# Latent attention on one Trainium2 core: probabilities transposed in two halves of 64 queries, with TensorE's four passes written out

## The chip, the cores and the metric

The kernel runs on one core of a Trainium2 chip. The metric is device time in microseconds (us), lower is better. The engines are TensorE (PE in the rows; PEld is its weight load), VectorE (DVE), ScalarE (ACT), GpSimd (POOL) and the DMA queues that SyncE (SP) feeds. They run side by side and wait for each other on semaphores. TensorE multiplies a stationary tile (loaded first, a "weight load") with a moving tile and writes to PSUM, which has eight banks (`ps_all[:, 0..7, :]`, 512 fp32 columns each); ScalarE and VectorE read PSUM.

## The reference, cut to what matters

The whole program is two transformer blocks at a width of 1024, with 512 tokens and, in the second block, 256 context tokens. The change concerns one stage only, the latent attention (`mla_mixer`) at the start of the second block, with 16 heads:

```python
def dense_attention(q_lat, q_ctx, k_lat, v_lat, k_ctx, v_ctx):
    ...
        s = jnp.concatenate([jnp.einsum('bqhd,bkhd->bhqk', qc, k_ctx),
                             jnp.einsum('bqhd,bkhd->bhqk', ql, k_lat)], -1)
        p = softmax_f32(s.astype(jnp.float32) * scale).astype(v_lat.dtype)
        return (jnp.einsum('bhqk,bkhd->bqhd', p[..., :n_ctx], v_ctx)
                + jnp.einsum('bhqk,bkhd->bqhd', p[..., n_ctx:], v_lat))

def ctx_attention(q, k, v):
    s = jnp.einsum('bqhd,bkhd->bhqk', q, k).astype(jnp.float32) * q.shape[-1] ** -0.5
    p = softmax_f32(s).astype(v.dtype)
    return jnp.einsum('bhqk,bkhd->bqhd', p, v)
```

The 512 latent queries see 256 context keys and 512 latent keys (768 keys). The 256 context queries see the 256 context keys. A query and key have 64 plain and 32 rotated dimensions, a value has 64.

## The kernel before

The program is a list of stages. Each engine runs its own instruction stream in a written order, and counting semaphores tie the streams together. The stage "mla" has four passes of four heads each. A pass first makes queries, keys and values from the compressed inputs, and then goes through twelve *pairs* (`MLA_PAIRS`). A pair is two heads (`g` = 0 and 1) with one block of 128 queries: for each of two head pairs (`hp`) four latent blocks with 768 keys (pairs 0 to 3 and 6 to 9) and two context blocks with 256 keys (4, 5, 10 and 11).

A pair goes through these steps:

- `scores(n)` on TensorE writes the scores of both heads to banks 0 to 3. The two heads stand in different halves (64 rows) or quarters (32 rows) of the array's rows.
- `most(n, g)` on VectorE takes the row maximum. `exps(n, g)` on ScalarE makes the exponentials `prob` and their sum. `shares(n, g)` on VectorE writes `diag`, a 128 by 128 diagonal of 1 over the sum.
- `turn(n, g)` on TensorE multiplies each 128 by 128 block of `prob` (stationary) with `diag` (moving), which transposes and normalises in one go. A latent head has six blocks. Before the change the first three go to bank 4 and the last three to bank 5, and a context head has two blocks in bank 4 alone.
- `copy(n, g)` brings the result to `prob_t` in SBUF: ScalarE copies bank 4 (semaphore `copied0`), VectorE bank 5 (`copied1`).
- `weigh(n)` on TensorE multiplies `prob_t` with the values.

TensorE's order is `scores(n + 1)`, `weigh(n - 1)`, `turn(n, 0)`, `turn(n, 1)`. ScalarE's is `exps(n + 1, 0)`, `copy(n, 0)`, `exps(n + 1, 1)`, `copy(n, 1)`. VectorE's is `most(n + 1, 0)`, `most(n + 1, 1)`, `copy(n, 0)`, `shares(n + 1, 0)`, `shares(n + 1, 1)`, `copy(n, 1)`. A turn may write a bank when the previous head's copy out of that bank is done.

On every engine the first three passes are one hardware loop and the last pass is written out (`Chain.loop`). In the loop the value of a wait comes from registers.

In the rows, L1545 to L1551 are the latent `scores` and L1540 and L1542 the context ones; L1562 and L1567 are `turn` into banks 4 and 5, L1582 is `weigh`, L1068 `exps`, L1078 ScalarE's copy, L2281 and L2282 `most`, L2261 and L2262 `shares`, and L2292 VectorE's copy. One fp32 matmul of the program is two records in the trace, each with its own weight load, so that "x6" is three matmuls. L1738 is a sum in another stage, whose moving tile is one column wide.

Of the kernel before, what the change touches and what calls it, by code (L numbers as in the profile page):

```python
# [238 lines left out]
def mla_step(a):  # L239
    wq, wkv = weight_panels(a["mla_w_qb_2"][0]), weight_panels(a["mla_w_kvb_2"][0])  # L240
    n = NH // PER
    pairs, units, lat = PER // 2 * 6, PER * 6, PER * 4

    def dma(i, j):

        w, per, first, second = ((wq, DQ, NOPE, ROPE), (wkv, P, NOPE, HD))[j]
        out = []
        for h in range(PER):
            out.append((("cols", h * first, first), w[:, :, ds(i * (PER * per) + h * per, first)]))
            out.append((("cols", PER * first + h * second, second), w[:, :, ds(i * (PER * per) + h * per + first, second)]))  # L250
        return out

    return dict(kind="mla", iters=n, shapes=[(3, PER * DQ), (2, PER * P)], dma=dma,
                totals=dict(q_mm=2 * n, q_out=3 * n, rot_mm=n, q_rot=n, key_mm=2 * n, val_mm=n, kv_out=4 * n,
                            s_made=pairs * n, s_max=units * n, s_exp=units * n, s_shared=units * n,
                            turned0=units * n, turned1=lat * n, copied0=units * n, copied1=lat * n,
                            s_weighted=pairs * n, s_kept=PER * n))
# [121 lines left out]
def build(nc, a, out, upto=99, probe=False):  # L379
# [133 lines left out]
    diag = sb("diag", [P, 2, 2, P], at=g_raw_at + 6144)  # L513
    prob_t = sb("prob_t", [P, 2, T], at=spare)
    prob = (sb("prob_even", [P, 2, T], at=spare + 6144), sb("prob_odd", [P, 2, T], at=g_raw_at + 8192))
    o_lat = sb("o_lat", [P, KD, S], at=hid)
# [515 lines left out]
    MLA_PAIRS = [(hp, ctx, q) for hp in range(PER // 2) for ctx, n in ((0, 4), (1, 2)) for q in range(n)]  # L1032
    MLA_LAT = [2 * sum(1 for u in MLA_PAIRS[:n] if not u[1]) for n in range(len(MLA_PAIRS))]

    def mla_act(st, b, act, split_hi, i, last):
        base_of = lambda name, per: b[name] + i * per
        U, LU = 2 * len(MLA_PAIRS), 4 * PER

# [18 lines left out]
        def exps(n, g):  # L1057
            hp, ctx, q = MLA_PAIRS[n]
            act.wait_ge(sem["s_max"], base_of("s_max", U) + 2 * n + g + 1)
            if n >= 2:  # L1060

                act.wait_ge(sem["turned0"], base_of("turned0", U) + 2 * n + g - 3)
                if not MLA_PAIRS[n - 2][1]:
                    act.wait_ge(sem["turned1"], base_of("turned1", LU) + MLA_LAT[n - 2] + g + 1)
            at = 8 * (n % 2) + 4 * g
# [5 lines left out]
        def copy(n, g):  # L1071
            hp, ctx, q = MLA_PAIRS[n]
            act.wait_ge(sem["turned0"], base_of("turned0", U) + 2 * n + g + 1)
            if n >= 1:

                act.wait_ge(sem["s_weighted"], base_of("s_weighted", len(MLA_PAIRS)) + n)
            W = (2 if ctx else 3) * P
            nc.scalar.activation(prob_t[:, g, 0:W], ps_all[:, 4, 0:W], ACT.Copy).then_inc(sem["copied0"], 1)  # L1078

# [382 lines left out]
    def mla_pe(st, b, pe, triple, i):  # L1462
        base_of = lambda name, per: b[name] + i * per
        U, LU = 2 * len(MLA_PAIRS), 4 * PER
        p0 = st["p0"]
# [88 lines left out]
        def turn(n, g):  # L1554
# [5 lines left out]
            pe.wait_ge(sem["copied0"], base_of("copied0", U) + u)  # L1560
            for t in range(2 if ctx else 3):
                ins = nc.tensor.matmul(ps_all[:, 4, t * P:(t + 1) * P], prob[n % 2][:, g, t * P:(t + 1) * P], diag[:, n % 2, g, :], start=True, stop=True)  # L1562
            ins.then_inc(sem["turned0"], 1)
            if not ctx:
                pe.wait_ge(sem["copied1"], base_of("copied1", LU) + MLA_LAT[n] + g)
                for t in range(3, 6):
                    ins = nc.tensor.matmul(ps_all[:, 5, (t - 3) * P:(t - 2) * P], prob[n % 2][:, g, t * P:(t + 1) * P], diag[:, n % 2, g, :], start=True, stop=True)  # L1567
                ins.then_inc(sem["turned1"], 1)

        def weigh(n):  # L1570

            hp, ctx, q = MLA_PAIRS[n]
            pe.wait_ge(sem["copied0"], base_of("copied0", U) + 2 * n + 2)
            if not ctx:
                pe.wait_ge(sem["copied1"], base_of("copied1", LU) + MLA_LAT[n] + 2)
            if q == 0 and hp == 1:
# [118 lines left out]
    def _(pe):  # L1695
# [123 lines left out]
        for st in PLAN:  # L1819
# [168 lines left out]
            elif kind == "mla":  # L1988
                Chain(pe, None).loop(st["iters"], 0, lambda i, last: mla_pe(st, b, pe, triple, i))
            elif kind == "na":  # L1990
# [275 lines left out]
    def mla_dve(st, b, dve, ch, i):  # L2266
        V = nc.vector
        base_of = lambda name, per: b[name] + i * per
        U, LU = 2 * len(MLA_PAIRS), 4 * PER
        dve.wait_ge(sem["rot_mm"], base_of("rot_mm", 1) + 1)  # L2270
# [13 lines left out]
        def copy(n, g):  # L2284
            hp, ctx, q = MLA_PAIRS[n]
            if ctx:
                return
            dve.wait_ge(sem["turned1"], base_of("turned1", LU) + MLA_LAT[n] + g + 1)
            if n >= 1:

                dve.wait_ge(sem["s_weighted"], base_of("s_weighted", len(MLA_PAIRS)) + n)
            V.tensor_copy(prob_t[:, g, 3 * P:T], ps_all[:, 5, 0:3 * P]).then_inc(sem["copied1"], 1)  # L2292

# [297 lines left out]
```

## Time and profile before

| | |
|---|---|
| median of 3 runs | 4306.83 us (4305.85 to 4313.46) |
| profiled execution, its own time | 4306.24 us |
| span of its trace | 4304.5 us |
| mean granted TensorE clock | 0.959 of full speed |
| TensorE matmul busy | 3925.6 us (91% of the span) |
| VectorE, ScalarE, GpSimd busy | 2144.8, 1398.0 and 1505.0 us |

The span runs from the first to the last instruction of the trace, and the profiled execution's own time has 1.7 us more around it. Busy time counts pipelined matmuls by their modelled ends, so that 91% does not mean a full array. The latent attention's pairs run in four stretches between 2194 and 2591 us.

### The profile page before, as it was taken

Reading aid. Unit: us, or ns where it says so; the run is one execution under the profiler, and the core shown is the slowest. Engines: PE = TensorE matmul, PEld = TensorE weight load, DVE = VectorE, ACT = ScalarE, POOL = GpSimd, SP = SyncE. Lnnn points to the kernel's source line nnn. Section 1 sums busy time; section 2 is a strip of 40 time slices with the busy share of each in tenths; the row PEclk is TensorE's granted clock in tenths of the full one; section 3 lists DMA queues with packets and bytes.
Section 4 is the critical chain, followed back from the end, with each engine's and each line's share of the span. In section 5 each row is a group of like instructions: output and inputs, shape, how many; then the busy total and the mean of one; then the engine's idle time right before and its main releaser. Section 6 shows DMA issues by size and latency. Waiting matters only on the chain.

```text
span 4304.5 us, 56639 instructions
## 1 busy us (share of the span) xinstructions
PE 3925.6 (91%) x20925; PEld 3254.3 (76%) x20925; DVE 2144.8 (50%) x3528; ACT 1398.0 (32%) x1862; POOL 1505.0 (35%) x494
## 2 busy tenths in 40 slices
PE   6999979999999978999989998799968889888997
PEld 5888868888888867888866667578758878767885
DVE  6344855445444677565454445776752332334232
ACT  3322343223412332312333331332234433234232
POOL 1443323343444321444310003344346633234441
PEclk9999989999999988999989998999979999999998
DMA  5454514444453323443300003244414422212221
GB/s 180 142 159 136 148 55 140 139 152 139 144 157 111 118 68 113 139 152 109 76 16 11 19 1 108 78 123 148 139 54 141 137 55 63 68 51 68 88 94 53
DMA packets 551756, 440.60 MB, mean 102 GB/s; under 512 B 60332, under 2 KB 549821, under 8 KB 551357
## 3 DMA queue, kind: packets, MB, share of 16 engines
q1 hardware_dynamic: 551613, 438.67, 33.1%
q8 instruction: 93, 1.52, 0.2%
q14 instruction: 50, 0.41, 0.0%
HBM read 431.58 MB, written 2.83 MB: 101 GB/s over the span
## 4 chain that ended last, share of the span: by engine, by line
PE 70%; DVE 14%; issue 7%; ACT 4%; DMA 2%; POOL 1%; SPq 1%; DVEq 0%; ACTq 0%; POOLq 0%
PE ps_all L1814 19%; PE ps_all L1816 18%; PE ps_all L1815 18%; DVE acc L2376 3%; PE ps_all L1562 2%; PE ps_all L1582 1%; PE ps_all L1879 1%; DMA g_raw<-in_w_mod_dram 1%; PE ps_all L1664 1%; PE ps_all L1567 1%; PE ps_all L1545 1%; DVE full_t L2433 1%; PE ps_all L1549 1%; ACT w_hi L1174 1%; POOL w_lo L789 1%
## 5 line engine op out<-in xcount | busy, mean ns | idle before, releaser
L789 POOL TENSOR_TENSOR w_lo<-raw,w_hi 128x2048 fp32r<-128x2048 f32 (+4 forms) x326 | 1343.1, 4121 | 2352.2 <-ACT w_hi L1174 2252.2
L1814 PE MATMUL ps_all<-h_hi,w_hi 128*128 128x512 f32 (+1 forms) x2704 | 1072.6, 397 | 43.9 <-POOL h_lo L795 34.9
L1815 PE MATMUL ps_all<-h_lo,w_hi 128*128 128x512 f32 (+1 forms) x2704 | 1059.1, 392 | 0.0
L1816 PE MATMUL ps_all<-h_hi,w_lo 128*128 128x512 f32 (+1 forms) x2704 | 1058.8, 392 | 0.0
L1174 ACT ACTIVATE w_hi<-raw 128x2048 fp32r<-128x2048 f32 (+4 forms) x320 | 537.8, 1681 | 1599.1 <-PE ps_all L1816 1424.6
L1814 PEld LDWEIGHTS ps_all<-h_hi,w_hi 128*128 128x128 f32 x2704 | 517.9, 192 | 156.4 <-issue 26.9
L2376 DVE SCALAR_TENSOR_TENSOR acc<-g_raw,c_col,acc 128x256 f32<-128x256 f32 x1104 | 618.2, 628 | 1.7
L1816 PEld LDWEIGHTS ps_all<-h_hi,w_lo 128*128 128x128 f32 x2704 | 516.9, 191 | 106.9
L1815 PEld LDWEIGHTS ps_all<-h_lo,w_hi 128*128 128x128 f32 x2704 | 517.8, 192 | 102.7 <-issue 1.0
L1814 PE MATMUL ps_all<-hid_hi,w_hi 128*128 128x512 f32 (+1 forms) x1272 | 482.3, 379 | 28.9 <-DVE hid_lo L2454 18.9
L1815 PE MATMUL ps_all<-hid_lo,w_hi 128*128 128x512 f32 (+1 forms) x1272 | 474.0, 373 | 0.0
L1816 PE MATMUL ps_all<-hid_hi,w_lo 128*128 128x512 f32 (+1 forms) x1272 | 473.9, 373 | 0.0
L1814 PEld LDWEIGHTS ps_all<-hid_hi,w_hi 128*128 128x128 f32 x1272 | 244.5, 192 | 73.0 <-DVE hid_lo L2454 21.0
L2454 DVE TENSOR_TENSOR hid_lo<-prod_t,hid_hi 128x1024 f32 (+3 forms) x77 | 229.2, 2977 | 110.7 <-ACT hid_hi L1268 110.7
L2451 DVE TENSOR_TENSOR prod_t<-gate_t,ps_all 128x1024 f32<-128x1024 f32 x44 | 53.8, 1222 | 449.7 <-PE ps_all L1816 449.7
L1816 PEld LDWEIGHTS ps_all<-hid_hi,w_lo 128*128 128x128 f32 x1272 | 244.8, 192 | 41.3
L1815 PEld LDWEIGHTS ps_all<-hid_lo,w_hi 128*128 128x128 f32 x1272 | 245.1, 193 | 40.2 <-issue 1.0
L2471 DVE SCALAR_TENSOR_TENSOR x<-ps_all,modc,x 128x512 f32 (+1 forms) x92 | 68.9, 748 | 316.0 <-PE ps_all L1816 315.9
L2378 DVE TENSOR_SCALAR acc<-g_raw,c_col 128x256 f32<-128x256 f32 x240 | 91.0, 420 | 125.2 <-DMA g_raw<-in_ada_w_dram 32.1
L1814 PE MATMUL ps_all<-c_hi,w_hi 128*128 128x256 f32 x400 | 120.1, 300 | 27.2 <-POOL w_lo L789 16.3
L2281 DVE TENSOR_REDUCE stat<-ps_all 128x1 f32<-128x768 f32 (+1 forms) x96 | 74.8, 779 | 125.9 <-PE ps_all L1551 114.4
L2225 DVE SCALAR_TENSOR_TENSOR prod_t<-ps_all,colv,prod_t 128x511 f32<-128x511 f32 (+1 forms) x66 | 40.6, 656 | 177.2 <-ACT prod_t L1263 177.2
(341 smaller groups left out, 5205.1 us busy)
## 6 DMA issues: line engine op xcount, KB each, us to landing
raw<-in_w_ffn_gu_dram SPq DMA_DIRECT2D x88, 1024.0 KB, 5.1
g_raw<-in_w_mod_dram SPq DMA_DIRECT2D x72, 1024.0 KB, 5.1
raw<-in_ffn_w_in_dram SPq DMA_DIRECT2D x66, 1024.0 KB, 5.1
g_raw<-in_ada_w_dram SPq DMA_DIRECT2D x48, 1024.0 KB, 5.3
raw<-in_w_ffn_down_dram SPq DMA_DIRECT2D x32, 768.0 KB, 4.8
raw<-in_w_ffn_down_dram SPq DMA_DIRECT2D x32, 640.0 KB, 4.4
raw<-in_ffn_w_out_dram SPq DMA_DIRECT2D x24, 768.0 KB, 4.8
raw<-in_ffn_w_out_dram SPq DMA_DIRECT2D x24, 640.0 KB, 4.4
```

The source lines that it names most:

```text
L789: nc.gpsimd.tensor_tensor(v(w_lo), v(raw), v(w_hi).bitcast(F32), ALU.subtract).then_inc(sem["w_split_lo"], 1)
L1174: nc.scalar.activation(w_view(w_hi, j % 2, st["shapes"][j]), w_view(raw, j % 2, st["shapes"][j]), ACT.Copy).then_inc(sem["w_split_hi"], 1)
L1562: ins = nc.tensor.matmul(ps_all[:, 4, t * P:(t + 1) * P], prob[n % 2][:, g, t * P:(t + 1) * P], diag[:, n % 2, g, :], start=True, stop=True)
L1814: nc.tensor.matmul(o, whi, mhi, start=first, stop=False)
L1815: nc.tensor.matmul(o, whi, mlo, start=False, stop=False)
L1816: return nc.tensor.matmul(o, wlo, mhi, start=False, stop=last)
L2281: ch.link(V.tensor_reduce(s_(0), pair[:, C:C + (C if ctx else T)], AX_X, ALU.max))
L2376: ins = nc.vector.scalar_tensor_tensor(o, w, s, o, ALU.mult, ALU.add)
L2378: ins = nc.vector.tensor_scalar(o, w, s, None, ALU.mult)
L2451: nc.vector.tensor_tensor(prod_t[:, :, 0:N], gate_t[:, :, 0:N], other, ALU.mult).then_inc(sem["product"], 1)
L2454: nc.vector.tensor_tensor(hid_lo[:, w].rearrange("p (c n) -> p c n", c=2), prod_t[:, :, 0:N], hid_hi[:, w].rearrange("p (c n) -> p c n", c ...
L2471: nc.vector.scalar_tensor_tensor(v, ps_d[:, j, 0:N], modc[:, ds(st["gate"] + j + i * 2, 1)], v, ALU.mult, ALU.add).then_inc(sem[f"down{j}" ...
```

## The change

In `turn`, each 128 by 128 block is now turned in two halves of 64 queries: rows 0 to 63 of `prob` with the upper left 64 by 64 of `diag`, and rows 64 to 127 with the lower right one. The first half (`qh` = 0) goes to bank 4, the second to bank 5, for all six blocks of a latent head and the two of a context head. ScalarE copies the first halves of all blocks from bank 4, VectorE the second halves from bank 5; `half_t` is the view of `prob_t` with every other run of 64 columns. Both banks now carry every head, so each turn and each `weigh` waits for both copies of the head before, and VectorE copies in context pairs too. On TensorE alone, the four passes are written out one after the other without a hardware loop; the other engines keep theirs.

```diff
 def mla_act
-            W = (2 if ctx else 3) * P
-            nc.scalar.activation(prob_t[:, g, 0:W], ps_all[:, 4, 0:W], ACT.Copy).then_inc(sem["copied0"], 1)
+            t = 2 if ctx else 6
+            nc.scalar.activation(half_t(g, 0, t), ps_all[:, 4, 0:t * HD].rearrange("p (t q) -> p t q", q=HD), ACT.Copy).then_inc(sem["copied0"], 1)
 def mla_pe, turn
             pe.wait_ge(sem["copied0"], base_of("copied0", U) + u)
-            for t in range(2 if ctx else 3):
-                ins = nc.tensor.matmul(ps_all[:, 4, t * P:(t + 1) * P], prob[n % 2][:, g, t * P:(t + 1) * P], diag[:, n % 2, g, :], start=True, stop=True)
-            ins.then_inc(sem["turned0"], 1)
-            if not ctx:
-                pe.wait_ge(sem["copied1"], base_of("copied1", LU) + MLA_LAT[n] + g)
-                for t in range(3, 6):
-                    ins = nc.tensor.matmul(ps_all[:, 5, (t - 3) * P:(t - 2) * P], prob[n % 2][:, g, t * P:(t + 1) * P], diag[:, n % 2, g, :], start=True, stop=True)
-                ins.then_inc(sem["turned1"], 1)
+            pe.wait_ge(sem["copied1"], base_of("copied1", U) + u)
+            for t in range(2 if ctx else 6):
+                for qh in range(2):
+                    rows_ = slice(qh * HD, (qh + 1) * HD)
+                    ins = nc.tensor.matmul(ps_all[:, 4 + qh, t * HD:(t + 1) * HD], prob[n % 2][rows_, g, t * P:(t + 1) * P], diag[rows_, n % 2, g, rows_], start=True, stop=True)
+                    if t == (1 if ctx else 5):
+                        ins.then_inc(sem[f"turned{qh}"], 1)
 weigh
-            if not ctx:
-                pe.wait_ge(sem["copied1"], base_of("copied1", LU) + MLA_LAT[n] + 2)
+            pe.wait_ge(sem["copied1"], base_of("copied1", U) + 2 * n + 2)
 tensor block
-                Chain(pe, None).loop(st["iters"], 0, lambda i, last: mla_pe(st, b, pe, triple, i))
+                for i in range(st["iters"]):
+                    mla_pe(st, b, pe, triple, i)
 def mla_dve, copy
-            if ctx:
-                return
-            V.tensor_copy(prob_t[:, g, 3 * P:T], ps_all[:, 5, 0:3 * P]).then_inc(sem["copied1"], 1)
+            t = 2 if ctx else 6
+            V.tensor_copy(half_t(g, 1, t), ps_all[:, 5, 0:t * HD].rearrange("p (t q) -> p t q", q=HD)).then_inc(sem["copied1"], 1)
```

The order of TensorE's rows around pair 1 of the looped passes was this (L1562 and L1567 are the two heads' turns, L1545 begins the next scores):

```order
L1562 MATMUL ps_all<-diag,prob_odd 128x128 [waits copied0,s_shared]
L1562 MATMUL ps_all<-diag,prob_odd 128x128 x2
L1567 MATMUL ps_all<-diag,prob_odd 128x128 [waits copied1]
L1567 MATMUL ps_all<-diag,prob_odd 128x128 x2
L1562 MATMUL ps_all<-diag,prob_odd 128x128 [waits copied0,s_shared]
L1562 MATMUL ps_all<-diag,prob_odd 128x128 x2
L1565 REGISTER_ALU
L1567 MATMUL ps_all<-diag,prob_odd 128x128 [waits copied1]
L1567 MATMUL ps_all<-diag,prob_odd 128x128 x2
L1533 REGISTER_ALU
L1545 MATMUL ps_all<-kn,qn 128x512 [waits s_exp]
```

In the changed kernel the same place reads as follows (L1564 is the turn, L1544 the scores):

```order
L1564 MATMUL ps_all<-diag,prob_odd 128x64 [waits copied1,copied0,s_shared]
L1564 MATMUL ps_all<-diag,prob_odd 128x64 x11
L1564 MATMUL ps_all<-diag,prob_odd 128x64 [waits copied1,copied0,s_shared]
L1564 MATMUL ps_all<-diag,prob_odd 128x64 x11
L1544 MATMUL ps_all<-kn,qn 128x512 [waits s_exp]
```

Six matmuls of 128 moving columns per head have become twelve of 64. The wait for the bank 5 copy, which stood in the middle of a head's turn, has moved to its front beside the wait for the bank 4 copy, and the register work is gone.

On VectorE, between the maxima and the shares of the context pairs, nothing was copied before (L2282 ends `most`, L2261 begins `shares`):

```order
L2281 TENSOR_REDUCE stat<-ps_all 128x1 [waits s_shared,s_made]
L82 REGISTER_ALU
L2282 TENSOR_SCALAR stat<-stat 128x1 [waits dve_chain]
L2260 REGISTER_ALU
L2261 RECIPROCAL stat<-stat 128x1 [waits s_exp]
```

Now a copy of 128 columns stands between them, and another behind the shares:

```order
L2279 TENSOR_REDUCE stat<-ps_all 128x1 [waits s_shared,s_made]
L82 REGISTER_ALU
L2280 TENSOR_SCALAR stat<-stat 128x1 [waits dve_chain]
L2289 COPY prob_t<-ps_all 128x2x64 [waits s_weighted,turned1]
L2258 REGISTER_ALU
L2259 RECIPROCAL stat<-stat 128x1 [waits s_exp]
```

## Rows read from the trace of the kernel before

**Rows 1.** The page: the chain that ended last, share of the span by engine.
```profile
PE 70%; DVE 14%; issue 7%; ACT 4%; DMA 2%; POOL 1%; SPq 1%; DVEq 0%; ACTq 0%; POOLq 0%
```

**Rows 2.** Windows, pass 3: length; busy PE, PEld, DVE, ACT, POOL; clock; DMA.
```profile
2407.00:2486.00 79.00, 72.23 (x593) 51.63 (x594) 37.15 (x106) 29.93 (x73) 2.34 (x1) 0.98 0.04 13
```

**Rows 3.** Timeline of PE (start us, length us), one latent pair of pass 4.
```profile
2560.59 1.13 PE L1545 MATMUL ps_all<-kn,qn 64*128 64x512 f32 x4
...
2563.57 1.53 PE L1582 MATMUL ps_all<-prob_t,vals 128*64 128x128 f32 x24
2565.03 0.94 PE L1562 MATMUL ps_all<-diag,prob_odd 128*128 128x128 f32 x6
...
2566.63 0.91 PE L1562 MATMUL ps_all<-diag,prob_odd 128*128 128x128 f32 x6
...
2568.15 1.13 PE L1545 MATMUL ps_all<-kn,qn 64*128 64x512 f32 x4
```

**Rows 4.** Timeline of PE and PEld: one-column matmuls; four loads into two row halves.
```profile
687.23 1.39 PE L1738 MATMUL ps_all<-mean_m,squares 128*128 128x1 f32 x12
2204.20 0.30 PEld L1545 LDWEIGHTS ps_all<-kn,qn 64*128 64x128 f32 x4
```

**Rows 5.** Groups of PE and PEld, 2150 to 2620 us, by form: busy us, mean ns.
```profile
L1567 PE MATMUL ps_all<-diag,prob_odd 128*128 128x128 f32 x192 | 26.7, 276 | 0.0
L1567 PEld LDWEIGHTS ps_all<-diag,prob_odd 128*128 128x128 f32 x192 | 24.0, 192 | 0.0
L1582 PEld LDWEIGHTS ps_all<-prob_t,vals 128*64 128x64 f32 x896 | 47.9, 137 | 18.8 <-issue 15.5 <-ACT prob_t L1078 3.3
```

**Rows 6.** Timeline of a looped pass, all engines: turns and copies of one pair.
```profile
2209.41 0.83 PE L1567 MATMUL ps_all<-diag,prob_odd 128*128 128x128 f32 x6
2209.69 0.49 ACT L1078 ACTIVATE prob_t<-ps_all 128x384 f32<-128x384 f32 x1
2210.28 0.56 DVE L2292 COPY prob_t<-ps_all 128x384 f32<-128x384 f32 x1 [0.77 <-PE ps_all L1567]
2210.33 0.91 PE L1562 MATMUL ps_all<-diag,prob_odd 128*128 128x128 f32 x6
```

**Rows 7.** Groups of ACT and DVE, 2150 to 2620 us: ScalarE's short copy, VectorE's diagonal.
```profile
L1078 ACT ACTIVATE prob_t<-ps_all 128x256 f32<-128x256 f32 x32 | 12.2, 382 | 17.8 <-PE ps_all L1562 17.8
L2262 DVE TENSOR_SCALAR diag<-ident,stat 128x128 f32<-128x128 f32 x96 | 27.6, 287 | 3.6 <-DVE stat L2261 0.2
```

**Rows 8.** Timeline of PE: context pairs 4 and 5 of pass 1, then scores.
```profile
2228.11 0.71 PE L1562 MATMUL ps_all<-diag,prob_even 128*128 128x128 f32 x4
2229.46 0.68 PE L1562 MATMUL ps_all<-diag,prob_even 128*128 128x128 f32 x4 [0.64 <-ACT prob_t L1078]
...
2233.64 0.71 PE L1562 MATMUL ps_all<-diag,prob_odd 128*128 128x128 f32 x4
2235.76 0.68 PE L1562 MATMUL ps_all<-diag,prob_odd 128*128 128x128 f32 x4 [1.41 <-ACT prob_t L1078]
2236.55 2.05 PE L1545 MATMUL ps_all<-kn,qn 64*128 64x512 f32 x4
```

**Rows 9.** Windows: the stretch that begins with those scores.
```profile
2236.60:2240.00 3.40, 3.40 (x10) 1.62 (x12) 0.38 (x2) 0.26 (x1) 0.00 (x0) 0.50 0.02 5
```

**Rows 10.** Timeline of PE: second scores and last weighing of passes 2, 3, 4.
```profile
2310.04 1.13 PE L1545 MATMUL ps_all<-kn,qn 64*128 64x512 f32 x4
2380.92 0.66 PE L1582 MATMUL ps_all<-prob_t,vals 128*64 128x128 f32 x8 [0.47 <-ACT prob_t L1078]
2415.86 1.13 PE L1545 MATMUL ps_all<-kn,qn 64*128 64x512 f32 x4
2485.10 0.66 PE L1582 MATMUL ps_all<-prob_t,vals 128*64 128x128 f32 x8 [0.47 <-ACT prob_t L1078]
2521.23 1.13 PE L1545 MATMUL ps_all<-kn,qn 64*128 64x512 f32 x4
2589.73 0.66 PE L1582 MATMUL ps_all<-prob_t,vals 128*64 128x128 f32 x8 [0.47 <-ACT prob_t L1078]
```

More of the change, by code:

```diff
@@ L241, in mla_step @@
     n = NH // PER
-    pairs, units, lat = PER // 2 * 6, PER * 6, PER * 4
+    pairs, units = PER // 2 * 6, PER * 6
     def dma(i, j):
@@ L255, in mla_step @@
                             s_made=pairs * n, s_max=units * n, s_exp=units * n, s_shared=units * n,
-                            turned0=units * n, turned1=lat * n, copied0=units * n, copied1=lat * n,
+                            turned0=units * n, turned1=units * n, copied0=units * n, copied1=units * n,
                             s_weighted=pairs * n, s_kept=PER * n))
@@ L514, in build @@
     prob_t = sb("prob_t", [P, 2, T], at=spare)
+    half_t = lambda g, h, n: prob_t[:, g, 0:n * P].rearrange("p (t h q) -> p h t q", h=2, q=HD)[:, h, :, :]
     prob = (sb("prob_even", [P, 2, T], at=spare + 6144), sb("prob_odd", [P, 2, T], at=g_raw_at + 8192))
@@ L1032, in build @@
     MLA_PAIRS = [(hp, ctx, q) for hp in range(PER // 2) for ctx, n in ((0, 4), (1, 2)) for q in range(n)]
-    MLA_LAT = [2 * sum(1 for u in MLA_PAIRS[:n] if not u[1]) for n in range(len(MLA_PAIRS))]
     def mla_act(st, b, act, split_hi, i, last):
         base_of = lambda name, per: b[name] + i * per
-        U, LU = 2 * len(MLA_PAIRS), 4 * PER
+        U = 2 * len(MLA_PAIRS)
         act.wait_ge(sem["q_mm"], base_of("q_mm", 2) + 1)
@@ L1062, in exps @@
                 act.wait_ge(sem["turned0"], base_of("turned0", U) + 2 * n + g - 3)
-                if not MLA_PAIRS[n - 2][1]:
-                    act.wait_ge(sem["turned1"], base_of("turned1", LU) + MLA_LAT[n - 2] + g + 1)
+                act.wait_ge(sem["turned1"], base_of("turned1", U) + 2 * n + g - 3)
             at = 8 * (n % 2) + 4 * g
@@ L1463, in mla_pe @@
         base_of = lambda name, per: b[name] + i * per
-        U, LU = 2 * len(MLA_PAIRS), 4 * PER
+        U = 2 * len(MLA_PAIRS)
         p0 = st["p0"]
@@ L2268, in mla_dve @@
         base_of = lambda name, per: b[name] + i * per
-        U, LU = 2 * len(MLA_PAIRS), 4 * PER
+        U = 2 * len(MLA_PAIRS)
         dve.wait_ge(sem["rot_mm"], base_of("rot_mm", 1) + 1)
@@ L2285, in copy @@
             hp, ctx, q = MLA_PAIRS[n]
[L2286 to L2288 removed]
+            dve.wait_ge(sem["turned1"], base_of("turned1", U) + 2 * n + g + 1)
             if n >= 1:
                 dve.wait_ge(sem["s_weighted"], base_of("s_weighted", len(MLA_PAIRS)) + n)
[L2292 removed]
+            t = 2 if ctx else 6
+            V.tensor_copy(half_t(g, 1, t), ps_all[:, 5, 0:t * HD].rearrange("p (t q) -> p t q", q=HD)).then_inc(sem["copied1"], 1)
         def shares(n, g):
```

## The prediction

> **What bounds the kernel now.** I read the chain that ended last first: TensorE makes 70% of it [rows 1]. Then I read the stage that the change touches. In pass 3 TensorE is busy for 72.23 of 79.00 us, VectorE for 37.15 and ScalarE for 29.93 [rows 2]. So what counts here is TensorE's own stream and the waits in it. The timeline of one latent pair in the written-out pass shows that stream: scores at 2560.59, weighing at 2563.57, the two heads' turns at 2565.03 and 2566.63, the next scores at 2568.15 [rows 3]. The pair takes 7.56 us, and its turns 1.60 + 1.52 = 3.12 us of that. The whole stage has 32 latent pairs and 16 context pairs.
>
> **One head's turn before.** Twelve records of 128 moving columns. A group of six lasts 0.83 us [rows 6] and its last record 0.276 us [rows 5], so the spacing is (0.83 - 0.276) / 5 = 0.11 us, and twelve take 1.33 us. Until the second head's turn starts 1.60 us pass, because it waits for ScalarE's copy of bank 4. Behind the second head 1.52 us pass until the scores.
>
> **One head's turn after.** Twelve matmuls of 64 columns become 24 records, in twelve couples of one upper and one lower half. Two rows say what binds them. Records whose moving tile is one column wide, with the same 128-column stationary tile, come (1.39 - 0.276) / 11 = 0.10 us apart [rows 4], the last record counted as above. So a record with one column costs about what one with 128 costs: the weight load is the limit, and narrower moving tiles gain nothing. Do the two halves' loads run side by side? In the scores, four loads into two row halves take 0.30 us together, with 0.19 us for one [rows 4, 5], so three steps fit into 0.11 us: one step of 0.1 between the two loads of one half, and nothing between the halves. A couple therefore costs one load, 0.11 us, and a head 12 x 0.11 = 1.33 us, as before. I take 1.33.
>
> The Trainium skill says the same of the load (TensorE: Matmul & The Clock Gate, LDWEIGHTS): its time goes with the columns of the stationary tile and not with its rows. The trace agrees: a load of 64 columns takes 137 ns and one of 128 takes 192 [rows 5]. Its page TensorEngine Tiling (Array Packing), Instruction Overhead, warns against taking a tiling factor from a dimension that is already small, and this change takes it from the moving one too.
>
> **The wait.** Before, the second head's turn into bank 4 waited only for ScalarE's copy, which ran while the first head's other half streamed into bank 5. That cover is gone: the last record now fills both banks, and both copies start only then. After the first head's start: last couple at 11 x 0.11 = 1.22 us, its end 0.276 later, 0.04 until VectorE starts (L1567's group ends at 2209.41 + 0.83 = 2210.24, the copy starts at 2210.28), 0.56 for its copy, and 0.11 until TensorE starts (ScalarE's copy ends at 2209.69 + 0.49 = 2210.18, the next turn's load at 2210.30) [rows 6]. That makes 2.21 for 1.60 before. ScalarE's copy is shorter, 0.49, and starts at most 0.1 later, so VectorE's decides. The second head's turn takes 1.33. The 0.19 us beyond it before the scores passed while the array went from 128-row to 64-row tiles; the turn now uses 64-row tiles itself, and I keep 0.02 of them (keeping all of them would add 24 x 0.17 = 4 us). So 2.21 + 1.35 = 3.56 for 3.12, +0.44 us a pair. VectorE is free in time: it had idled 0.77 us before that copy [rows 6]. Behind its copy stand the shares of the next pair, which TensorE needs only after 2.98 us of scores and 1.46 of weighing (2560.59 to 2563.57 to 2565.03) [rows 3]; that cover holds.
>
> Of eight latent pairs in a pass, this hits six. In the first of each head pair (0 and 6) the second turn already stood still for ScalarE, whose copy is queued behind the next exponentials; there I take 0. So 24 x 0.44 = **+10.6 us**.
>
> **Context pairs.** Eight records before, now eight couples at the same spacing. The copy was exposed before too: the second turn starts at 2229.46, 1.35 after the first, with 0.64 idle for ScalarE [rows 8]. ScalarE's copy shrinks from 256 to 128 columns: 0.489 for 384 and 0.382 for 256 [rows 6, 7] give 0.11 us per 128, so 0.27; VectorE's new one of 128 columns takes about 0.29, as its diagonal of that width [rows 7]. Each exposed copy is 0.1 shorter, and before the scores at least another 0.1 goes. With two such savings in each of four pairs, 4 x 0.2 x 4 passes = **-3.2 us**.
>
> **Written-out passes.** From its second scores to its last weighing, pass 3 takes 2485.10 - 2415.86 = 69.24 us in the loop and pass 4 2589.73 - 2521.23 = 68.50 us written out [rows 10]. With the rest of a pass, 0.8 to 0.9 each in three passes: **-2.5 us**. On a longer instruction stream nothing in the trace puts a price; it is fetched during stretches of 100 us.
>
> These sum to 10.6 - 3.2 - 2.5 = +4.9 us.
>
> **The clock.** Pass 2 differs from pass 3 in one thing: its clock fell once behind the context pairs. It takes 2380.92 - 2310.04 = 70.88 us, 1.64 more [rows 10]. In pass 1 the same happened: two short turns with 1.41 us of waiting between them, and the scores behind them take 2.05 us instead of 1.13 [rows 8], at a granted clock of 0.50, which is 1.2 GHz [rows 9]. Two of the eight context groups did this. Such stretches become more and thinner: every steady latent pair now has turn, 0.87 us of waiting, turn, and the array streams half as many columns while it turns. From below this costs nothing. From above, all 24 steady latent pairs and the six other context groups fall once each, 30 x 1.64 = 49 us. I take the six context groups, whose stretch is the nearest to the row that fell, and four of the 24, 10 x 1.64 = **+16 us**.
>
> The sum is +21 us on the profiled execution's own 4306.24, 4327; the median of the runs is 0.6 us above that execution, which changes nothing.
>
> **The rivals.**
>
> *Wait without clock.* The wait comes as above and the clock falls little more often than before: +5 us, 4311. For it: pass 3's context groups did not fall at all. Against: pass 1's and 2's did, with more streaming than will be left.
>
> *The halves really run at twice the rate, and it is faster.* If a couple costs half a load, 0.055, the second head starts 0.60 + 0.99 = 1.59 us after the first (0.99 is the tail and the copy as above), and takes 0.68: 2.27 for 3.12, 24 x -0.85 = -20. The other eight latent pairs give 8 x -0.7 = -6, the context pairs -6, the written-out passes -2.5, some falls of the clock +8: -26, 4280. It decides below 0.09 us a couple, where 2 x 12 x 0.02 us pay for the 0.44. The Trainium skill's page TensorEngine Tiling (Array Packing), Theoretical Speedup, promises up to twofold for a contraction of 64 rows or fewer. For it: the scores of two heads do run together. Against: these scores stream 256 or 512 columns behind each load, and the one-column row puts the load at 0.10.
>
> *The halves' loads run one after the other.* A couple costs 0.22: 32 x 2 x 1.33 = +85 and 32 x 0.44 = +14 for the context turns, with the sum above about +104 before the clock, over 4410. Against it stand the four loads in 0.30 us.
>
> **How the numbers follow.** The wait with a falling clock 0.62, the wait alone 0.18, twice the rate 0.11, serial loads 0.06, something else (a copy that is slower into runs of 64 columns) 0.03. Predicted is the first, 4327 us. The range reaches from just below the second to past all 24 latent pairs falling, 4303 to 4358; outside are the third and fourth and some of the first's tail. What a measurement of this kernel can tell from no change is 0.2%, 8.6 us: faster 0.11 (the third), same 0.19 (the second), slower 0.70.
>
> **What the profile of the changed kernel would show.** The spacing of the turn's records at full clock, by group: 24 records in about 1.5 us is right, 0.9 speaks for twice the rate, 2.9 for serial loads. Between the two heads' turns, idle of some 0.7 us that ends with VectorE's copy. The second turn of a context pair 1.25 us behind the first instead of 1.35. More stretches at a granted clock of 0.50 between 2194 and 2600 us, behind turns. The prediction is wrong if the spacing is not the load's, or if the clock holds.

## The result and the profile after

The changed kernel takes 4381.78 us (median of 4 runs, 4381.18 to 4393.31) where the kernel before takes 4306.69 (4 runs, 4305.85 to 4313.46): a ratio of 1.0177, 95% interval 1.0164 to 1.0189, or 75 us more. The profiled execution's own time is 4381.38 us, its span 4379.6, its mean granted clock 0.941.

Windows of the latent attention from pass 1's first scores to pass 4's last weighing, before and after, then two stretches of the changed kernel in pass 1. The columns are length; busy PE, PEld, DVE, ACT, POOL with their instructions; clock; DMA share; GB/s.

```profile
2187.70:2590.80 403.10, 365.46 (x2781) 266.25 (x2780) 171.01 (x458) 154.40 (x338) 21.51 (x7) 0.96 0.04 10
```

```profile
2184.20:2672.80 488.60, 433.66 (x3677) 319.87 (x3676) 180.28 (x490) 151.67 (x338) 21.51 (x7) 0.78 0.03 9
2213.00:2227.00 14.00, 12.45 (x166) 9.89 (x163) 6.59 (x20) 4.36 (x11) 0.00 (x0) 0.98 0.01 3
2227.00:2233.00 6.00, 6.00 (x44) 4.37 (x42) 1.64 (x5) 1.05 (x3) 0.00 (x0) 0.50 0.00 0
```

The stage grew by 85.5 us and its clock went from 0.96 to 0.78. Summed over the trace's clock records, TensorE stood at half clock for 34 us in 6 stretches before and for 210 us in 24 stretches after, the longest 27.3 us. Outside this stage the profiled execution was 10 us shorter than before, with 310 us at half clock for 322. Over all kernels below, the time outside the stage lay between 3892 and 3910 us. Lengths of the stage therefore tell the small differences better than whole spans do, though each comes from a single profiled execution.

The timeline of PE, one latent pair at full clock in pass 1, which answers to [rows 3], with VectorE's copy between its turns; a context pair that answers to the second of [rows 8]; and the first context pair of pass 4, at full clock (start, length, x records, idle before and what ended it):

```profile
2216.70 1.56 PE L1564 MATMUL ps_all<-diag,prob_even 64*128 64x64 f32 x24
2218.33 0.56 DVE L2289 COPY prob_t<-ps_all 128x384 f32<-128x384 f32 x1 [0.76 <-PE ps_all L1564]
2219.03 1.56 PE L1564 MATMUL ps_all<-diag,prob_even 64*128 64x64 f32 x24 [0.78 <-DVE prob_t L2289]
2220.39 0.68 PE L1539 MATMUL ps_all<-kn,qcn 64*128 64x256 f32 x4
...
2237.80 0.66 PE L1564 MATMUL ps_all<-diag,prob_odd 64*128 64x64 f32 x8
2239.91 0.97 PE L1564 MATMUL ps_all<-diag,prob_odd 64*128 64x64 f32 x8 [1.45 <-DVE prob_t L2289]
...
2607.05 0.66 PE L1564 MATMUL ps_all<-diag,prob_even 64*128 64x64 f32 x8
2608.22 0.66 PE L1564 MATMUL ps_all<-diag,prob_even 64*128 64x64 f32 x8 [0.51 <-DVE prob_t L2289]
2608.68 1.11 PE L1544 MATMUL ps_all<-kn,qn 64*128 64x512 f32 x4
```

The groups of the four copies, which answer to [rows 6, 7]:

```profile
L2289 DVE COPY prob_t<-ps_all 128x384 f32<-128x384 f32 x64 | 35.7, 557 | 69.4 <-PE ps_all L1564 69.4
L1077 ACT ACTIVATE prob_t<-ps_all 128x384 f32<-128x384 f32 x64 | 31.4, 490 | 84.9 <-PE ps_all L1564 84.9
L2289 DVE COPY prob_t<-ps_all 128x128 f32<-128x128 f32 x32 | 9.3, 289 | 31.6 <-PE ps_all L1564 31.6
L1077 ACT ACTIVATE prob_t<-ps_all 128x128 f32<-128x128 f32 x32 | 8.8, 276 | 32.9 <-PE ps_all L1564 32.9
```

At full clock the mechanism is the one forecast. A head's 24 records last 1.56 us and the second head's turn starts 2.33 us after the first, with an idle time of 0.78 that VectorE's copy ends. What the forecast did not see is in the timeline of pass 3, where the clock falls in the middle of a pair; behind it stands the first pair of pass 1, whose turns run at half clock throughout:

```profile
2469.16 1.56 PE L1564 MATMUL ps_all<-diag,prob_even 64*128 64x64 f32 x24
2471.49 2.21 PE L1564 MATMUL ps_all<-diag,prob_even 64*128 64x64 f32 x24 [0.78 <-DVE prob_t L2289]
2473.43 1.24 PE L1539 MATMUL ps_all<-kn,qcn 64*128 64x256 f32 x4
...
2475.75 2.83 PE L1579 MATMUL ps_all<-prob_t,vals 128*64 128x128 f32 x24
2478.51 1.79 PE L1564 MATMUL ps_all<-diag,prob_odd 64*128 64x64 f32 x24
2481.08 1.60 PE L1564 MATMUL ps_all<-diag,prob_odd 64*128 64x64 f32 x24 [0.78 <-DVE prob_t L2289]
2482.44 1.21 PE L1539 MATMUL ps_all<-kn,qcn 64*128 64x256 f32 x4
...
2484.73 2.83 PE L1579 MATMUL ps_all<-prob_t,vals 128*64 128x128 f32 x24
2487.49 1.12 PE L1564 MATMUL ps_all<-diag,prob_even 64*128 64x64 f32 x8
```

```profile
2196.32 2.83 PE L1564 MATMUL ps_all<-diag,prob_even 64*128 64x64 f32 x24
2199.92 2.83 PE L1564 MATMUL ps_all<-diag,prob_even 64*128 64x64 f32 x24 [0.78 <-DVE prob_t L2289]
2202.50 2.06 PE L1544 MATMUL ps_all<-kn,qn 64*128 64x512 f32 x4
```

The weighing takes 2.83 us at half clock instead of 1.53, the context scores 1.24 instead of 0.68. The clock comes back during the turn at 2478.51 (1.79 us long, between the 1.56 of full clock and the 2.83 of half clock) and is gone again one turn later. Of the 24 stretches at half clock, 13 begin in one of the 24 *steady* latent pairs (1, 2, 3, 7, 8 and 9 of a pass), always behind the start of its second turn; before the change none did. Six begin in the context pairs (two before) and five at the start of a pass or in its first pair (four before).

### The profile page after: what moved, and what is told of

Its sections match the earlier page's. It is cut to its first block, busy times and chain, and to the rows that moved or that the text cites. A ratio compares the mean times of both kernels' runs of the same rounds, so it can differ in the third digit from the quotient of the medians.

```text
span 4379.6 us, 58255 instructions
## 1 busy us (share of the span) xinstructions
PE 3987.9 (91%) x21821; PEld 3302.1 (75%) x21821; DVE 2154.8 (49%) x3560; ACT 1395.8 (32%) x1862; POOL 1505.8 (34%) x494
## 3 DMA queue, kind: packets, MB, share of 16 engines
HBM read 431.58 MB, written 2.83 MB: 99 GB/s over the span
## 4 chain that ended last, share of the span: by engine, by line
PE 72%; DVE 13%; issue 7%; ACT 3%; POOL 2%; DMA 1%; SPq 1%; DVEq 0%; ACTq 0%; POOLq 0%
PE ps_all L1811 19%; PE ps_all L1813 18%; PE ps_all L1812 18%; DVE acc L2373 3%; PE ps_all L1564 3%; PE ps_all L1579 2%; POOL w_lo L790 1%; PE ps_all L1876 1%; DMA g_raw<-in_w_mod_dram 1%; PE ps_all L1544 1%; PE ps_all L1661 1%; PE ps_all L1548 1%; DVE full_t L2430 1%; PE ps_all L1720 1%; PE ps_all L1802 1%
```

## The experiments

"Half clock" below is the sum of the clock records at 0.50 inside the stage. The stage's length goes from the first scores of pass 1 to the start of the last record of the last weighing. Each kernel was timed against the kernel before on the same chip; the last column is that ratio with its 95% interval. Beside the experiments the kernel before took 4309 to 4311 us, so ratios and stages compare the rows better than medians do. "Thin" means 64 moving columns in a turn's matmul instead of 128.

| kernel | us, median | stage | half clock | ratio |
|---|---|---|---|---|
| before | 4306.69 | 402.4 | 34 | |
| changed | 4381.78 | 487.9 | 210 | 1.0177 [1.0164, 1.0189] |
| e1 before, passes written out | 4307.66 | 404.6 | 41 | 0.9994 [0.9984, 1.0004] |
| e2 e1 with both waits in front | 4323.18 | 421.4 | 37 | 1.0029 [1.0018, 1.0040] |
| e3 e1 with thin moving tiles | 4319.82 | 417.4 | 79 | 1.0025 [1.0015, 1.0035] |
| e9 e2 and e3 together | 4416.22 | 516.3 | 266 | 1.0241 [1.0223, 1.0259] |
| e4 changed, waits filled in 6 pairs | 4345.21 | 444.2 | 109 | 1.0080 [1.0063, 1.0097] |
| e7 changed, all waits filled | 4326.94 | 423.0 | 55 | 1.0040 [1.0025, 1.0056] |
| e12 and pass starts filled | 4301.11 | 400.7 | 0 | 0.9975 [0.9966, 0.9984] |
| e8 e1 with its gaps filled | 4297.32 | 389.7 | 0 | 0.9971 [0.9962, 0.9981] |
| e6 changed, loop restored | 4394.44 | 498.2 | 224 | 1.0206 [1.0187, 1.0226] |
| e5 changed, 64 by 64 quadrants | 4290.05 | 388.5 | 67 | 0.9957 [0.9942, 0.9973] |
| e10 quadrants, gaps filled | 4270.67 | 366.1 | 0 | 0.9908 [0.9894, 0.9922] |
| e11 and the steady waits filled | 4264.95 | 366.0 | 0 | 0.9893 [0.9876, 0.9910] |

### The passes written out (e1), the wait in front (e2) and thin tiles (e3)

e1 is the kernel before with only TensorE's passes written out:

```diff
-                Chain(pe, None).loop(st["iters"], 0, lambda i, last: mla_pe(st, b, pe, triple, i))
+                for i in range(st["iters"]):
+                    mla_pe(st, b, pe, triple, i)
```

> The kernel before with one thing changed: TensorE's four passes written out. Both theories below expect the same, three passes shorter by 0.8 to 0.9 us each: about 4304 us against 4306.7, and the same clock. If writing out costs instruction fetch on TensorE, it would be above 4310, and that would be a part of the 75 us.

e2 adds the wait for VectorE's copy at the front of each latent head's turn, with 128-row tiles:

```diff
             pe.wait_ge(sem["copied0"], base_of("copied0", U) + u)
+            if not ctx:
+                pe.wait_ge(sem["copied1"], base_of("copied1", LU) + MLA_LAT[n] + g)
...
-                pe.wait_ge(sem["copied1"], base_of("copied1", LU) + MLA_LAT[n] + g)
```

> Passes written out, blocks turned whole (128 moving columns), but each latent head's turn waits for both copies of the head before it at its front. This is the changed kernel's wait without its halves. Schedule alone: 24 pairs with some 0.6 us more and nothing saved before the scores, +14 - 2.5, 4318 us. Theory A (the clock falls because the turns stream half as many columns AND stand still between them; both are needed): few more stretches at half clock, 4318 to 4332. Rival B (the standing still alone brings the clock down): as the changed kernel, 4365 to 4385, with some 200 us at half clock in the stage.

e3 is e1 with half as many columns streamed behind each load, in bank 4 as shown and in bank 5 alike. It leaves out the right half of each turned block:

```diff
-... ps_all[:, 4, t * P:(t + 1) * P], prob[n % 2][:, g, t * P:(t + 1) * P], diag[:, n % 2, g, :], ...
+... ps_all[:, 4, t * P:t * P + HD], prob[n % 2][:, g, t * P:(t + 1) * P], diag[:, n % 2, g, 0:HD], ...
```

> Passes written out, waits as in the kernel before, but each turn's moving tile is only the left 64 columns of the diagonal, so that the other half of each turned block is left out (stale values are copied). This has the changed kernel's thin streaming without its wait. The spacing of the records should stay 0.11 us, so the schedule alone gives 4304. Theory A: few more stretches at half clock, 4304 to 4320. Rival C (thin streaming alone brings the clock down): 4360 or more.

The timeline of PE for e2, one latent pair of pass 4:

```profile
2540.52 0.94 PE L1564 MATMUL ps_all<-diag,prob_odd 128*128 128x128 f32 x6
2541.29 0.83 PE L1568 MATMUL ps_all<-diag,prob_odd 128*128 128x128 f32 x6
2542.87 0.91 PE L1564 MATMUL ps_all<-diag,prob_odd 128*128 128x128 f32 x6 [0.74 <-DVE prob_t L2294]
2543.61 0.83 PE L1568 MATMUL ps_all<-diag,prob_odd 128*128 128x128 f32 x6
2544.37 1.13 PE L1545 MATMUL ps_all<-kn,qn 64*128 64x512 f32 x4
```

and for e3, one of pass 1:

```profile
2211.39 0.88 PE L1562 MATMUL ps_all<-diag,prob_odd 128*128 128x64 f32 x6
2212.10 0.83 PE L1567 MATMUL ps_all<-diag,prob_odd 128*128 128x64 f32 x6
2213.02 0.85 PE L1562 MATMUL ps_all<-diag,prob_odd 128*128 128x64 f32 x6
```

And for e1 one latent pair of pass 1 and one of pass 4, with ScalarE's copy between the turns:

```profile
2208.27 0.94 PE L1562 MATMUL ps_all<-diag,prob_odd 128*128 128x128 f32 x6
2209.32 0.49 ACT L1078 ACTIVATE prob_t<-ps_all 128x384 f32<-128x384 f32 x1
2209.96 0.91 PE L1562 MATMUL ps_all<-diag,prob_odd 128*128 128x128 f32 x6
...
2539.22 0.94 PE L1562 MATMUL ps_all<-diag,prob_odd 128*128 128x128 f32 x6
2540.19 0.49 ACT L1078 ACTIVATE prob_t<-ps_all 128x384 f32<-128x384 f32 x1 [1.10 <-PE ps_all L1562]
2540.83 0.91 PE L1562 MATMUL ps_all<-diag,prob_odd 128*128 128x128 f32 x6
```

Written out, the passes gain nothing that a run can tell: the time is the same, and the stage is 2.2 us longer with 7 us more at half clock. The rows show why. In the first three passes the second turn still starts 1.69 us after the first, and in the fourth 1.61, just as in the kernel before. It waits for ScalarE's copy, which starts 1.05 us after the first turn there and 0.97 in pass 4. ScalarE still has its loop in e1, over passes 1 to 3.

e2 shows the bare wait: its pair takes 3.85 us for 3.12, the idle time of 0.74 ends with VectorE's copy, and no steady latent pair lost its clock; its 37 us lie in the first pairs of the passes. Its stage is 16.8 us longer than e1's.

In e3 the six records into bank 5 last 0.83 us as with 128 columns [rows 6], so what spaces records with a 128-column stationary tile is not the moving columns. Streaming half as many saves only about 0.06 us a turn: a steady pair's turns take 1.63 + 1.45 us in the first passes, e1's 1.69 + 1.51. Yet its stage is 12.8 us longer, with twice the half clock. Those stretches begin at the starts and ends of the passes and behind the context pairs; the steady latent pairs kept their clock.

### Both together (e9)

e9 joins the edits of e2 and e3, with whole 128-row tiles; it leaves out the same halves of each turned block as e3.

> The kernel before, passes written out, with both of the last two experiments' edits at once: waits for both copies at the front of a latent head's turn, and only the left 64 columns of the diagonal as moving tile (half of each turned block is left out). The stationary tiles keep 128 rows. Sum without interplay: +12.5 for the wait and +11 for the thin turns on 4308, 4331 us. Theory A (the clock needs both): like the changed kernel, 4375 to 4390 us, and about 200 us at half clock in the stage. If the changed kernel's loss came from 64-row tiles rather than from half as many columns, it would be 4331 to 4340.

Windows of e9's stage:

```profile
2188.90:2705.80 516.90, 460.57 (x2781) 334.52 (x2780) 170.71 (x458) 154.64 (x338) 21.51 (x7) 0.74 0.03 8
```

The wait alone made the stage 16.8 us longer and thin tiles alone 12.8, and together it is 111.7, with 266 us at half clock. That is also over the 4375 to 4390 us that were expected. So neither the split into row halves nor the second bank for context heads is needed for the loss: turns with 128-column loads, 64 streamed columns and a wait between them make it.

### Unused matmuls in the waits (e4, e7, e12, e8)

These kernels add matmuls whose result nobody reads. e4, in the changed kernel:

```diff
             for g in range(2):
                 turn(n, g)
+                if g == 0 and n in (1, 2, 3, 7, 8, 9):
...
+                    for r in range(3):
+                        nc.tensor.matmul(ps_all[:, 7, :], low_hi[:, 0, 0:P], low_hi[:, 1, 0:S], start=True, stop=True)
```

> The changed kernel with three matmuls of 512 columns added between the two heads' turns of the six steady latent pairs of a pass, where TensorE stands 0.78 us; their result goes to an idle bank and is not used. If the clock is the cost (A, B and C alike): most stretches at half clock go, 4320 to 4345 us, faster than the changed kernel although it does more work. If the 67 us beyond the schedule come from anything else, the time stays at 4382 or grows by 24 x 0.1 to 0.2 us to 4386.

e7 has `BETWEEN[n]` of them between the turns of each of the twelve pairs, with 256 columns in pairs 4, 5, 6, 10 and 11, and 3 ahead of each of the last two weighings of a pass; e12 puts 12 more at each pass's start. e8 is e1 with such matmuls at the start of a pass, in its first and seventh pair, in the context pairs and ahead of the last two weighings:

```diff
+        BETWEEN = (3, 3, 3, 3, 4, 11, 6, 3, 3, 3, 4, 4)    # e7
+        BETWEEN = (5, 3, 3, 3, 4, 11, 4, 3, 3, 3, 4, 4)    # e12, with fill(12, True) behind scores(0)
+        BETWEEN = (5, 0, 0, 0, 4, 11, 4, 0, 0, 0, 4, 4)    # e8, with fill(12, True) behind scores(0)
```

> The changed kernel with matmuls of no use in all of its waits inside the twelve pairs (between the heads' turns of all pairs, and ahead of the last two weighings), 256 or 512 columns each. Filling six of twelve pairs gave back 37 to 42 of 75 us and left 109 us at half clock, mostly behind the context pairs. If those are due to the waits too, they go as well: 60 us or less at half clock, and the schedule's own +10 with some +5 for the added work remains, 4318 to 4330 us. If the thin turns hold the clock down by themselves there, 4335 to 4345.

> The kernel before (whole blocks, its own waits), passes written out, with matmuls of no use in its own waits: 12 of 512 columns in the 3.33 us between the first two scores of each pass, 5 in the first pair, and of 256 columns in the context pairs and the seventh. The stage has 34 to 41 us at half clock, which cost about half of it. If filling holds the clock there, 41 us become under 10 and the time 4292 to 4300 against 4308 for the same kernel without; if the filling delays more than it gives, 4308 to 4315.

> The changed kernel with unused matmuls in all of its waits and 12 at each pass's start, where the kernel that filled the waits alone still had stretches of 17.1 us at half clock. The kernel of before with its own gaps filled in this way took 4297 us with a stage of 389.7 us and no half clock, so that the two now differ by the change's schedule alone, plus three unused matmuls between the turns of 24 latent pairs. Theory (the change costs its schedule, 0.57 us in 24 pairs, 3 us back in the context pairs, and all the rest is clock): no half clock in the stage, 13.7 - 3.2 = +10 us over those 4297, plus up to 5 us where the unused matmuls outlast the wait: 4307 to 4313 us, stage 400 to 405 us. Rival (something else of the change costs time even at full clock, such as VectorE's context copies or the strided output): stage above 410 us, over 4318 us.

Windows of e12's stage and then of e8's:

```profile
2190.20:2591.00 400.80, 398.36 (x3949) 298.25 (x3948) 180.17 (x490) 151.23 (x337) 21.55 (x7) 1.00 0.04 11
```

```profile
2192.80:2583.00 390.20, 382.52 (x2981) 285.95 (x2980) 171.41 (x458) 154.40 (x338) 21.57 (x7) 1.00 0.04 11
```

and e12's timeline of PE, a latent pair of pass 1:

```profile
2208.22 1.55 PE L1564 MATMUL ps_all<-diag,prob_odd 64*128 64x64 f32 x24
2209.70 0.96 PE L1586 MATMUL ps_all<-low_hi 128*128 128x512 f32 x3
2210.60 1.56 PE L1564 MATMUL ps_all<-diag,prob_odd 64*128 64x64 f32 x24
2211.99 1.08 PE L1544 MATMUL ps_all<-kn,qn 64*128 64x512 f32 x4
```

e4 fills the waits of six latent pairs per pass and halves the half clock, from 210 to 109 us; what is left begins at pass starts, in the first pair and in or behind the context pairs. With those waits filled too, e7 keeps 55 us, nearly all of it 17.1 us at the start of three of the passes.

e12 does everything that the changed kernel does and more, and it takes 81 us less: its stage holds the full clock from end to end and is 87.2 us shorter, for 210 us at half clock taken away. That is 0.41 us lost per microsecond at half clock.

e12 and e8 both stand at full clock, both are written out, and their stages differ by 400.7 - 389.7 = 11.0 us. This is what the change's schedule costs, 24 x 0.08 = 1.9 us of it the unused matmuls that outlast the wait (a steady pair's turns take 2.38 + 1.39 us, not 2.33 + 1.36). By whole runs the two are only 4 us apart, 4301.11 and 4297.32, and e12 came out 6 us below its expected 4307 us while its stage lay in the expected range. Outside the stage e12's profiled execution was 12.6 us shorter than e8's, with 306 us at half clock for 343.

### The loop restored (e6)

The edit undoes e1's in the changed kernel.

> The changed kernel with TensorE's three first passes as a hardware loop again, halves as they are. Theory (the written-out passes are worth about 3 us in either kernel and have no part in the clock): 4383 to 4388 us, half clock in the stage 200 to 230 us. Rival (the loop's pauses or the code loading of a written-out stream are part of the loss): more than 10 us away from 4381.8 us in either direction, with the first three passes differing in length from the fourth.

It took 4394.44 us, 12.7 over the changed kernel in the medians, where the theory expected 1 to 6. The rival's bound of 10 us is passed, but its second sign is missing: from first scores to last weighing the passes took 109.3, 102.6, 106.1 and 108.5 us, so the looped three are no different from the fourth, and its steady pairs at full clock take 2.33 + 1.36 us as in the changed kernel. Half clock rose by 14 us, which at 0.41 is 6 of the stage's 10.3. Of these 10.3 us, 8.6 lie between the passes (71.7 us in three gaps for 63.1), where half clock rose from 12.2 to 22.5 us. It stays open why the clock fell more there, and whether the loop costs something between passes besides.

### Quadrants (e5, e10, e11)

e5 cuts the changed kernel's halves again, by keys, so that each matmul loads 64 columns into one quarter of the array:

```diff
+                for kh in range(2):
                     for qh in range(2):
-                    ... ps_all[:, 4 + qh, ...], prob[n % 2][rows_, g, t * P:(t + 1) * P], ...
+                    ... ps_all[keys_, 4 + qh, ...], prob[n % 2][rows_, g, t * P + kh * HD:t * P + (kh + 1) * HD], ...
```

> The changed kernel with each half block cut once more by keys: four matmuls of 64 rows, 64 stationary and 64 moving columns for a 128 by 128 block, in four quarters of the array. My theory of the turn (the load of the 128-column stationary tile is its limit, 0.11 us; a 64-column one takes 0.055): four quarters side by side take 0.055 to 0.06, a head 0.7 instead of 1.33 us, the pair 3.69 - 1.3 = 2.4 us, and the array streams densely again: 4270 to 4300 us. Rival (records are issued no faster than the weighing's, one each 0.055 us): four take 0.22, a head 2.6, 4450 us or more.

e10 adds e8's unused matmuls to it, and e11 two more in each steady latent pair.

> The quadrant kernel, plus unused matmuls of 512 or 256 columns in the waits at the start and end of each head pair and around the context pairs (5 between the turns of pair 0; 4, 11 and 4 in pairs 4 to 6; 4 and 4 in 10 and 11; 12 at the start of a pass; 3 before a context weighing), none between the turns of the steady latent pairs. In the quadrant kernel the half clock lasted 66.7 us of the stage, in stretches of 13.7, 6.8, 10.2, 6.8, 10.2, 6.8, 10.2 us that all lie at the start and end of passes or behind context pairs. Theory (the steady pairs with 0.80 us of waiting and 48 thin matmuls per head hold the full clock by themselves, only the gaps between passes and groups lose it): these falls go away, 66.7 x 0.43 = -28 us, against about 7 us for the unused matmuls at pass starts (from the kernel with the halves as before and the same filling, which gained 10 us for 17 of clock): 4269 us, half clock in the stage under 10 us. Rival (the thin turns hold the clock only by chance of where the falls lie, and longer full stretches move the falls into steady pairs): 4285 to 4295 us.

> As the kernel before in this batch, with two unused 512-column matmuls more between the two heads' turns of each of six latent pairs per pass (1, 2, 3, 7, 8, 9). Theory (steady pairs need no help): same time as without them or up to 24 x 0.1 = 2 to 5 us more, because switching the tile size of the array twice costs something; 4269 to 4275 us. Rival (steady pairs need the help): faster than the kernel without them by 5 us or more.

The timeline of PE for e5, a latent pair of pass 1, and then the window that stands beside the changed kernel's 2213 to 2227:

```profile
2216.55 0.93 PE L1565 MATMUL ps_all<-diag,prob_even 64*64 64x64 f32 x48
2218.27 0.93 PE L1565 MATMUL ps_all<-diag,prob_even 64*64 64x64 f32 x48 [0.80 <-DVE prob_t L2290]
2219.13 0.70 PE L1539 MATMUL ps_all<-kn,qcn 64*128 64x256 f32 x4
```

```profile
2213.00:2227.00 14.00, 12.40 (x294) 9.17 (x290) 8.06 (x24) 5.38 (x14) 0.00 (x0) 1.00 0.01 3
```

and e11's timeline with the filled wait:

```profile
2215.77 0.73 PE L1587 MATMUL ps_all<-low_hi 128*128 128x512 f32 x2
2216.64 0.93 PE L1565 MATMUL ps_all<-diag,prob_odd 64*64 64x64 f32 x48
2217.50 0.70 PE L1539 MATMUL ps_all<-kn,qcn 64*128 64x256 f32 x4
```

48 records of a quarter each take 0.93 us where 24 of a half took 1.56. The Trainium skill (TensorEngine Tiling (Array Packing), Key Properties) says that different tiles load weights and multiply in parallel, and this trace agrees, with about 0.015 us of spacing per record ((0.93 - 0.24) / 47). Its table (Theoretical Speedup) gives up to 2x where one dimension is small. The trace agrees in so far as a couple of halves takes 0.11 us, where two loads at that spacing, one behind the other, would take 0.22. But the blocks turned before had no small dimension, with a contraction of 128 rows, and against them row halves with 128 stationary columns gained nothing; the gain came only when the stationary tile shrank too. The pair takes 1.72 + 0.86 = 2.58 us for 3.12 before, with the whole exposed wait still in it. The wait is as long as the changed kernel's (0.80 for 0.78), and its steady pairs hold the clock. So 64 streamed columns and a wait are not enough to lose it; in the kernels that lost it, a turn also lasted about 1.5 us and not 0.93. Why that should matter, no run shows. What half clock e5 has, 67 us, begins at the starts and ends of passes, and e10 removes it all: 4270.67 us where 4269 was expected. e11's median is 5.7 us below e10's, which by the number alone passes the rival's 5 us, but its stage is as long as e10's (366.0 and 366.1): the profiled executions differ by 6 us outside the stage, and steady pairs need no help. Both are about 1% faster than the kernel before and faster than the changed one by over 110 us.

## Why the prediction was wrong

The forecast was +21 us, 4327 us, in a range of 4303 to 4358; it became +75 us, 4381.78. The direction was right, and the cause of the larger part was named, the clock, but its size lay outside the range.

**One head's turn: right.** The forecast was 1.33 us, bound by the load. 24 records last 1.56 us, less about 0.28 for the last one's end, in twelve steps of 0.11. Rivals "twice the rate" (0.9 us) and "serial loads" (2.9 us) are excluded by that row. e3 changed the moving columns and kept the spacing, e5 halved the stationary ones and halved it, so the stationary columns are the limit.

**The wait: right, slightly small.** VectorE's copy was named, and it took 557 ns where 0.56 was taken. The pair's turns take 2.33 + 1.36 = 3.69 us, forecast 3.56: the copy starts 1.63 us after the first turn and not 1.54, and the second turn 0.14 us after the copy's end and not 0.11. The base of 3.12 us came from pass 4, while the same turns took 1.69 + 1.51 = 3.20 us in the first three passes. So the wait cost 6 x 0.57 + 18 x 0.49 = 12.2 us, for 10.6.

**Context pairs and copies: right.** The copies of 128 columns took 0.289 and 0.276 us for the 0.29 and 0.27 taken. At full clock, in pass 4, the second turn of pair 4 starts 1.17 us after the first, where 1.28 was the time before in that pass and 1.25 the forecast. e12 against e8 gives the whole schedule, wait and context pairs, as 11.0 - 1.9 = +9.1 us once the filling is taken off. With the 12.2 us of the wait, that leaves -3.1 for the rest, where -3.2 was forecast for the context pairs.

**The written-out passes: wrong cause.** The -2.5 us came from pass 3 against pass 4 and was put down to TensorE's loop. (The scores that [rows 10] calls second are the third of their pass; the lengths are right.) e1 shows no gain that can be told (0.9994, interval to both sides of 1), and the difference stays when TensorE has no loop: from a pass's third scores to the end of its last weighing, the kernel before takes 69.89 us in pass 3 and 69.16 in pass 4, and e8 69.83 in each of the first three passes and 69.17 in the fourth. It goes with ScalarE's copy, which in the three passes where ScalarE loops starts 0.08 us later in a steady pair. In the changed kernel VectorE's copy ends the wait, and the pairs take 3.69 us in all four passes; that is the 0.49 above.

**The clock: this step failed.** It was given +16, from ten falls that each cost 1.64 us, 4 of them in the 24 steady latent pairs, and 49 us as its upper bound. It measured (210 - 34) x 0.41 = 72 us. Three things were wrong in it. The number of stretches rose by 18, to 24, not by ten: 13 in steady pairs where four were taken, four more in context pairs where six were taken, and one more in the first pair of a pass. The cost of one, 1.64 us, was taken from a single stretch of 3.4 us at half clock that dense work followed. Per microsecond that is 0.48, near the 0.41 measured. But here a stretch lasted 210 / 24 = 8.8 us on average and up to 27.3, so that even 18 falls would have come to 30 us at that price. And the upper bound rested on the same unit price, so that counting all 24 pairs still fell short. The prediction priced every fall by itself, as if the next pair stood at full clock again. In the changed kernel the work behind a fall is another thin turn and another wait; that this is why the clock stayed down so long is not shown by itself. What e2, e3 and e9 do show is that the two together are far more than their sum: +16.8 and +12.8 us of stage alone, +111.7 together.

The terms as measured, 12.2 - 3.1 + 72 = 81 us, stand against the stage's 85.5, and 4.4 us stay open; the filling in e12 makes the price of 0.41 slightly too low. The price comes from the same kernels as the sum, so the sum is no second test of it. The direction and the mechanism held, and the term that was mis-sized is the clock's, by a factor of four and a half.

## What to carry to other kernels

Split matmuls over parts of the array only as far as the stationary tile shrinks with them: if the load of 128 columns is what spaces the records, half the rows and half the moving columns save next to nothing, and quarters of 64 by 64 do (1.56 to 0.93 us). Before a difference between a looped and a written-out pass is put down to one engine's loop, look which engine ends the wait. Before an edit adds a wait between short bursts, or thins a burst next to a wait, price the clock as a state of the whole stretch and not as a count of single falls: the changed stage stood at half clock for 210 of its 488 us. A filled wait is a cheap test of such a suspicion, and can even be worth keeping: with its passes written out, the kernel before became 10 us faster (4307.66 to 4297.32 us) through matmuls whose result nobody reads.

## What the runs showed of the hardware

- The rows' busy time does not tell whether the clock holds. In the windows from 2213 to 2227 us above, TensorE was busy for 12.45 us in the changed kernel, whose clock fell at their end to 0.50, and for 12.40 us in the quadrant kernel, whose clock stayed at 1.00, with waits between the turns of 0.78 and 0.80 us. The quadrant kernel's turns last 0.93 us and not 1.56; that this is what holds its clock is not shown.
- Idle gaps alone do not tell either. The Trainium skill (TensorE: Matmul & The Clock Gate, A second HAM failure mode: psum-queue depth-cycling) describes brief idling between groups of matmuls that makes the clock oscillate. The changed kernel's trace agrees, with 24 stretches at half clock; e2, with waits of 0.74 us between dense turns, does not, with 37 us of half clock in all and none in its steady latent pairs.
- Half clock costs 0.41 us per microsecond in this stage (87.2 us for 210). At half clock throughout, the turns of a latent pair take 3.60 + 2.58 = 6.18 us for 3.69, which is 0.40 lost per microsecond. Part of the reason is that the wait for VectorE's copy is 0.78 us at either clock. Where filling at pass starts brought the clock back, the gain was smaller, 14.9 us for 41 in e8 and 22.4 for 67 in e10, with the filling's own cost in it.
- Four 64 by 64 quarters of the array take their loads and their matmuls side by side: 48 records last 0.93 us, about 0.015 us per record and 0.06 for four, where one load of 64 columns over all rows, in the weighing, comes every 0.054 us ((1.53 - 0.28) / 23). Row halves with 128-column loads stay at 0.11 us per couple, 0.055 per record.
